# Merge gates as one product of 1024 columns, six pairs of k-tiles by Strassen's seven block products

## The reference, cut to what matters

```
u = rmsnorm(x, norm_w)
proj = u @ w_in                      # 4096 x 24576: a_q a_f a_i a_g c_b c_c c_h c_g (2048 each), g_a g_b (4096 each)
y_a = rmsnorm(hgrn2(a_q, a_f, a_i)) * silu(a_g)
y_b = (c_b * conv3(c_c * c_h)) * silu(c_g)
merged = sigmoid(g_a + bias0) * (y_a @ w_branch_a) + sigmoid(g_b + bias1) * (y_b @ w_branch_b)
out = rmsnorm(x + merged @ w_out, final_norm_w)
```

## Time and profile before

| | us |
|---|---|
| three runs | 2910.37 to 2911.72, median 2911.26 |
| the profiled execution | 2910.26 |
| its span (first to last instruction) | 2908.5 |
| TensorE busy in the span | 2889.1 |
| VectorE busy | 1600.1 |
| ScalarE busy | 1231.9 |
| one merge, period | 131.5 |

### The profile page before, as it was taken

The page is one execution under the profiler, slowest core; times in us unless marked ns, Lnnn a source line. Parts: engine busy times, 40 slices in busy tenths (PEclk is TensorE's granted clock), DMA queues, the critical chain, the costliest instruction groups (busy, mean ns, idle before and its releaser), DMA issues.

```text
span 2908.5 us, 39078 instructions
## 1 busy us (share of the span) xinstructions
PE 2889.1 (99%) x13155; PEld 2399.5 (82%) x13155; DVE 1600.1 (55%) x1794; ACT 1231.9 (42%) x1326; POOL 6.7 (0%) x22
## 2 busy tenths in 40 slices
PE   8999999999999999999999999999999999999998
PEld 7888888888888888888888888888888888888886
DVE  6566666666665554555554454445454454555454
ACT  5443444344434444444444344443444344444443
POOL 0000000000000000000000000000000000000000
PEclk9999999999999999999999999999999999999999
DMA  7555555555556666666566666666666666666665
GB/s 240 181 180 167 174 174 179 166 177 174 176 170 192 192 190 190 192 192 191 189 193 201 195 196 195 197 197 193 196 194 197 194 197 194 197 201 212 219 202 202
DMA packets 426970, 556.63 MB, mean 191 GB/s; under 512 B 25393, under 2 KB 287650, under 8 KB 426914
## 3 DMA queue, kind: packets, MB, share of 16 engines
q1 hardware_dynamic: 426914, 555.90, 61.4%
HBM read 551.61 MB, written 4.19 MB: 191 GB/s over the span
## 4 chain that ended last, share of the span: by engine, by line
PE 99%; DVE 0%; ACT 0%; DMA 0%; ACTq 0%; DVEq 0%; issue 0%; SPq 0%
PE PS L837 32%; PE PS L839 32%; PE PS L838 32%; PE SC L868 1%; PE SC L845 0%; PE SS L868 0%; DMA XS<-in_x 0%; DVE WS L483 0%; PE SS L845 0%; PE OB L878 0%; PE OB L877 0%; PE SC L858 0%; PE OB L876 0%; PE SC L899 0%; PE SC L891 0%; PE SC L907 0%
## 5 line engine op out<-in xcount | busy, mean ns | idle before, releaser
L483 DVE TENSOR_TENSOR WS<-RAW,WS 128x1024 fp32r<-128x1024 f32 x1024 | 1253.7, 1225 | 1247.9 <-ACT WS L314 1226.6
L314 ACT ACTIVATE WS<-RAW 128x1024 fp32r<-128x1024 f32 x1024 | 1084.6, 1060 | 1617.4 <-PE PS L839 1613.6
L837 PE MATMUL PS<-WS,U 128*128 128x512 f32 x3584 | 1408.2, 393 | 2.8 <-DVE WS L483 2.8
L839 PE MATMUL PS<-WS,U 128*128 128x512 f32 x3584 | 1397.3, 390 | 0.0
L838 PE MATMUL PS<-WS,U 128*128 128x512 f32 x3584 | 1396.7, 390 | 0.0
L839 PEld LDWEIGHTS PS<-WS,U 128*128 128x128 f32 x3584 | 673.5, 188 | 140.9
L837 PEld LDWEIGHTS PS<-WS,U 128*128 128x128 f32 x3584 | 673.8, 188 | 140.0 <-issue 3.0
L838 PEld LDWEIGHTS PS<-WS,U 128*128 128x128 f32 x3584 | 674.0, 188 | 135.8
L839 PE MATMUL PS<-WS,Y 128*128 128x512 f32 x512 | 199.4, 389 | 0.0
L837 PE MATMUL PS<-WS,Y 128*128 128x512 f32 x512 | 199.4, 389 | 0.0
L838 PE MATMUL PS<-WS,Y 128*128 128x512 f32 x512 | 199.3, 389 | 0.0
(11 more groups left out here) (158 smaller groups left out, 585.6 us busy)
## 6 DMA issues: line engine op xcount, KB each, us to landing
RAW<-in_w_in SPq DMA_DIRECT2D x1024, 256.0 KB
RAW<-in_w_in SPq DMA_DIRECT2D x256, 512.0 KB
RAW<-in_w_out SPq DMA_DIRECT2D x128, 512.0 KB
RAW<-in_w_branch_a SPq DMA_DIRECT2D x64, 512.0 KB
RAW<-in_w_branch_b SPq DMA_DIRECT2D x64, 512.0 KB
XS<-in_x SPq DMA_DIRECT2D x8, 512.0 KB, 5.5
BIAS<-in_gate_bias SPq DMA_DIRECT2D x16, 256.0 KB, 3.8
XR<-in_x SPq DMA_DIRECT2D x8, 512.0 KB, 4.5
```

The source lines that it names most:

```text
L314: act.activation(WS[s][:, :, 0:OW], RAW[s][:, :, :], ACT.Copy).then_inc(hi_ready, 1)
L483: dve.tensor_tensor(WS[s][:, :, OW:2 * OW], RAW[s][:, :, :], WS[s][:, :, 0:OW], ALU.subtract).then_inc(lo_ready, 1)
L837: pe.matmul(bank, top, w[:, k, 0:OW], start=at_k == 0, stop=False)
L839: op = pe.matmul(bank, low, w[:, k, 0:OW], start=False, stop=at_k == n_tiles - 1)
```

## The change

Gates a and b of a merge become one stream of 16 **units**. A unit is a pair of k-tiles (j, j+16) by 1024 columns (512 of g_a and 512 of g_b): two loads of 512 KB, each one k-tile by 2x512 columns. Ten units are plain (N): four blocks of 128x512 of weights, six matmuls each, 24 in all, summed in the new PSUM tile `QL` (4 banks, in the place of `SC`, `OB`, `SS`). Six units are seven block products (S): the 2x2 blocks (row half by k-tile) times (k-tile by gate) are multiplied in Winograd's form with seven products of three matmuls, 21 in all. The activation sums for them (`SV`, and x21 - x22 in the place of x21's k-tile 0 to 5) are made once, in the last branch; the weight sums on DVE in every S unit. Units come in the order NNSNNSNSNNSNSNSN; the split weights lie in a ring `QS` of 11 blocks, and `block_used` counts the blocks that TensorE has used. Products common to several outputs are collected in `PS[0]` and `PS[1]` and added by `gates_early` and `gates_late`.

Since sums mix the two row halves, the rows must be scaled beforehand: during and after the first branch `U` is rebuilt as (high + low) times 1/rms and split again, in five batches of k-tiles; drains after that are plain copies or products.

`merged` rows go to a DRAM tensor instead of being transposed in the next merge; in the last merge seven of them are loaded back (`MB`), transposed and split. The first merge and the last are written out beside the loop. `x_rms` gets two small multiplications of the identity by 1/rms and TensorE one product with ones, from which a row of 1/rms (`RB`) is made. In the cut below, arguments are shortened where they don't matter; `gates_early` ends with four more additions of 512 columns with a drain after each.

```diff
+UNITS: "NNSNNSNSNNSNSNSN"; N_SEVEN = 6; QRING = 11; AHEAD_UNITS = 2
+NORM_BATCHES = ((0, 8), (8, 16), (16, 24), (24, 28), (28, 32))
# SP
+            def merge(i, first=False, last=False):
+                for u, (_, j) in enumerate(UNITS):
+                    for h in range(2):
+                        load_gates(i, j + KH * h, 2 * u + h, chunk + 2 * u + h)     # waits lo_ready, chunk - 3
+                    if u == 5 and not first:
+                        sp.wait_ge(merged, i)
+                        sp.dma_start(M_DRAM[i - 1], GA).then_inc(spilled, 16)
+                    if u == 9:
...
+                        sp.dma_start(GA[:, 0, :], gate_bias[0, 0, cols].partition_broadcast(P)).then_inc(bias_loaded, 16)
+                        sp.dma_start(GB[:, 0, :], gate_bias[0, 1, cols].partition_broadcast(P)).then_inc(bias_loaded, 16)
                 for n, w in enumerate((w_branch_a, w_branch_b)):
                     for c in range(CB):
                         load_wide(w[0], (i + 1) * OW - OW, c, chunk + 2 * CD + n * CB + c)
+                        at_c = n * CB + c
+                        if last and at_c >= 4 and at_c % 2 == 0:
+                            for m in ((0, 1, 2, 3) if at_c == 4 else (at_c // 2 + 1,) if at_c < 12 else ()):
+                                if m == 0:
+                                    sp.wait_ge(w_used, chunk + 2 * CD)
+                                if m >= 4:
+                                    sp.wait_ge(m_turned, m - 3)
+                                sp.dma_start(MB[m % 4][:, :, :], M_DRAM[m]).then_inc(m_back[m % 4], 16)
# DVE, first branch (ACT: norm_hi copies the high part, 1024 or 2048 columns a batch)
+            def norm_scale(n):
+                dve.wait_ge(w_used, CD + (b + 1) // KC)
+                after()
+                dve.tensor_tensor(t, U[:, a:b, 0:T], U[:, a:b, T:2 * T], ALU.add)
+                after()
+                dve.tensor_tensor(t, t, RB[:, :]..., ALU.mult).then_inc(u_scaled, 1)
+            def norm_lo(n):
+                dve.wait_ge(u_norm_hi, n + 1)
+                dve.tensor_tensor(U[:, a:b, T:2 * T], NT[n % 2]..., U[:, a:b, 0:T], ALU.subtract).then_inc(u_norm, 1)
+                    if first and slot in (10, 12, 14):
+                        norm_scale((slot - 10) // 2)
+                    if first and slot in (11, 13, 15):
+                        norm_lo((slot - 11) // 2)
+                    if last and slot == 10:
+                        seven_sums()          # 8 operations of 768 columns
+                    if last and slot == 12:
+                        seven_lo()
+                if first:                     # after slot 15
+                    norm_scale(3); norm_lo(3); norm_scale(4); norm_lo(4)
# DVE, S unit
+            def seven(i, u, n_th):
+                for t in (s, s + 1):
+                    dve.wait_ge(raw_loaded[t], ...)
+                    dve.wait_ge(block_used, (N_BLOCKS - 1) * i + (n + 6 - QRING + 1))
+                dve.tensor_tensor(two sums, 1024 columns).then_inc(t_sum, 1)
+                after()
+                dve.tensor_tensor(sums[2], sums[0], w22, ALU.add)
+                after()
+                dve.tensor_tensor(sums[3], sums[2], w21, ALU.add).then_inc(t_sum, 1)
+                dve.wait_ge(hi_ready, chunk + 2)
+                dve.tensor_tensor(low parts of 3 blocks).then_inc(lo_ready, 2)
+                for m in range(2):
+                    dve.wait_ge(t_hi, ...)
+                    dve.tensor_tensor(low parts of 2 sums).then_inc(t_ready, 1)
+            def gates_early(i):               # before the lo of the first w_branch_a chunk
+                dve.tensor_tensor(GA[:, 0, :], GA[:, 0, :], GB[:, 0, :], ALU.add)
+                after()
+                dve.wait_ge(block_used, (N_BLOCKS - 1) * i + (FIRST[LAST_S] + 6))
+                dve.tensor_tensor(GB[:, 0, :], a, GB[:, 0, :], ALU.add)
+                dve.tensor_tensor(GA[:, 0, :], e, GA[:, 0, :], ALU.add)
+                after()
...
+            def gates_late(i):                # before the lo of chunk 2
+                dve.wait_ge(w_used, MERGE_CHUNK + MERGE * i + 2 * CD)
+                dve.tensor_tensor(GA[:, :, :], QL[:, 0:2, :], GA[:, :, :], ALU.add)
+                dve.tensor_tensor(GB[:, :, :], QL[:, 2:4, :], GB[:, :, :], ALU.add).then_inc(drained, 1)
+                    lo(chunk + 2 * CD + c, c % RING)
+                    if last and c >= 7 and c % 2 == 1:
+                        turned_lo((c - 7) // 2)     # two operations of 512 columns; ACT: turned_hi after the same hi
+                    if first and 2 <= u < 5:
+                        convolve(NP - 1, u - 2, PS[0][:, 0, :], PS[0][:, 1, :], held=True)   # step 0 increments conv_read
# TensorE
+                        if n_th == 0:         # first S unit
+                            if first:
+                                pe.wait_ge(conv_read, NP)
+                    if last and c % 2 == 0 and c >= 2 * CD + 2:
+                        n = (c - 2 * CD - 2) // 2
+                        if n < NM - 1:
+                            if n > 0: pe.wait_ge(m_ready, n)      # turned_lo(n - 1) is through
+                            pe.wait_ge(m_back[n % 4], n // 4 * 16 + 16)
+                            turn_merged(n, MB[n % 4])
```

More of the change, by code:

```diff
@@ L148, in build @@
         u_ready = sem("u_ready")
+        rms_ready = sem("rms_ready")
+        rms_spread = sem("rms_spread")
+        u_scaled = sem("u_scaled")
+        u_norm_hi = sem("u_norm_hi")
+        u_norm = sem("u_norm")
+        v_sums = sem("v_sums")
+        v_hi = sem("v_hi")
+        v_ready = sem("v_ready")
+        t_sum = sem("t_sum")
+        t_hi = sem("t_hi")
+        t_ready = sem("t_ready")
+        block_used = sem("block_used")
+        conv_read = sem("conv_read")
+        spilled = sem("spilled")
+        m_back = [sem(f"m_back{i}") for i in range(4)]
         fq_turned = sem("fq_turned")
@@ L398, in merge @@
                 group = MERGE_GROUP + 4 * i
[L399 to L420, removed]
+                act.wait_ge(v_ready, 1)
+                n_th = 0
+                for u, (kind, _) in enumerate(UNITS):
+                    if u < AHEAD_UNITS:
+                        continue
+                    if kind == "S":
+                        seven(i, u, n_th)
+                        n_th += 1
+                    else:
+                        for h in range(2):
+                            plain(i, u, h)
@@ new lines, in merge @@
+                for c in range(2 * CB + RING):
+                    if c < RING:
+                        after_gates(i, c)
+                    else:
+                        hi(chunk + 2 * CD + c, c % RING)
+                    if c == RING:
+                        act.wait_ge(drained, group + 2)
+                        act.activation(GA[:, :, :], GA[:, :, :], ACT.Sigmoid).then_inc(merge_gate, 1)
+                        act.activation(GB[:, :, :], GB[:, :, :], ACT.Sigmoid).then_inc(merge_gate, 1)
+                    if last and c >= 7 and c % 2 == 1 and c < 2 * CB + RING + 1:
+                        turned_hi((c - 7) // 2)
@@ L422, in _, with turned_hi @@
+            def turned_hi(n):
+                act.wait_ge(m_turned, n + 1)
+                for j in range(2):
+                    op = act.activation(U[:, 4 * n + 2 * j:4 * n + 2 * j + 2, 0:T], pair(SC[j]), ACT.Copy)
+                op.then_inc(m_hi, 1)
             merge(0, first=True)
@@ L431, in output @@
                         if first and n == 0 and c == MERGED_AT + 2:
[L432 to L435, removed]
+                            turned_hi(NM - 1)
                     if last and n == 1:
@@ L952, in _, with three @@
                 branch(i, CONV_CHUNK, CONV_GROUP, is_conv=True, conv_of=i - 1)
[L954 to L960 removed]
+            def three(bank, top, low, q, start, stop):
+                w = QS[:, q % QRING, :]
+                pe.matmul(bank, top, w[:, 0:OW], start=start, stop=False)
+                pe.matmul(bank, top, w[:, OW:2 * OW], start=False, stop=False)
+                return pe.matmul(bank, low, w[:, 0:OW], start=False, stop=stop)
@@ new lines, in gates @@
+            def gates(i, first):
+                pe.wait_ge(v_ready, 1)
+                pe.wait_ge(y_ready, 2 * NP - 1)
+                pe.wait_ge(drained, MERGE_GROUP + 4 * i - 2)
+                n_th = 0
+                for u, (kind, j) in enumerate(UNITS):
+                    if kind == "S":
+                        if n_th == 0:
+                            pe.wait_ge(drained, MERGE_GROUP + 4 * i)
+                            if first:
+                                pe.wait_ge(conv_read, NP)
+                        seven(i, u, j, n_th)
+                        n_th += 1
+                    else:
+                        plain(i, u, j)
+                    if first and u == 0:
+                        turn_conv(NP - 1, PS[0][:, 0, :], PS[0][:, 1, :])
```

396 lines of the change are left out of this document (293 added, 103 removed).

## The result

The changed kernel takes 2916.64 us (median of 20 runs, 2914.51 to 2921.0) against 2910.78 (20 runs) before: ratio 1.002, 95% interval 1.0014 to 1.0027. That is 5.9 us slower: small, just at the 0.2% that the prediction called distinguishable, but the interval leaves out 1. The prediction's range held the time; its 2913 was 3.6 us short. The profiled execution's span went from 2908.5 to 2915.5 us, by 7.0.

The account below looks back on a forecast made before the run. TensorE bounds the kernel: number of matmuls times 0.2267 us. -32.6 + 14.0 + 0.6 + 0 + 3.0 + 2.0 + 14.9 = +1.9 us, so 2913 us ("the same", chance 0.40); range 2901 to 2929, by its own bounds 2903 to 2923.

Parts of the forecast that it names:

- The gain, 32.6 us: Gates of 8 merges: 21 matmuls for 24 in each S unit, 144 matmuls saved at 0.2267 us, 32.6 us faster.
- block ends cost TensorE: Rival, slower: 656 blocks each change bank and increment a semaphore; 20 ns each is 13 us, 2926; chance 0.10 with other losses.
- S units at no cost: Pairs SN: VectorE works 9.1 of 10.2 us and stays ahead, cover 0.65; loads take 5.2 of 5.7 us; cost 0.
- S units come late: Rival, slower, at the 48 S units: VectorE's slack or load pairs fall short, half a microsecond at tight pairs, 2925; chance 0.26.
- First branch, 14.0: Normalization in the first branch: x_rms 0.5, 11.9 us waited at second branch's chunk 4, slow matmuls behind it 1.6; sum 14.0.
- Last branch 0.6: seven_sums in slot 10 takes VectorE 7.7 us; the `lo` behind it is ready at 11.5, wanted at 10.9: 0.6 us.
- end of the gates 3.0: After each merge's last plain unit, gates_early delays the first w_branch_a chunk's `lo`: 0.4 us each, 8 times, 3.0 (bounds 0 and 8).
- First merge, 2.0: TensorE's first S unit waits for conv_read, as VectorE does its own S unit and two PSUM copies first: 2.0 us.
- Last merge, 14.9: Six turn_merged wait for turned_lo, 1.1 us each; three wait longer for loads, 4.2, 3.7, 3.7: 14.9 (bounds 6.7 and 19).
- a slower clock after these pauses is absorbed: Last merge: slow matmuls behind its pauses add nothing to the 14.9, since the load ends last.
- Eight such at 0.20 more cost 1.6: Behind the first branch's 11.9 us wait, TensorE starts slowly: eight matmuls at 0.20 us more, 1.6 (bounds 0 and 3).
- the row with 0.6 us of idle: Profile row at x_rms where TensorE already waits 0.60 us; after that pause no slow start of matmuls was seen.

Follow-up runs that it names:

- three_of_16: Changed kernel with three units by block products instead of six (375 gate matmuls a merge instead of 366): 2927.9 us, ratio 1.0061 to the kernel before.
- mb_later: Changed kernel with the loads of merged rows 4, 5 and 6 issued two chunks later in the last merge: 2910.89 us, ratio 1.0 to the kernel before.
- last_fix: Changed kernel with merged-row loads two chunks later and each turn_merged one chunk later in the last merge: 2901.02 us, ratio 0.9963 to the kernel before.
- two_sevens: Changed kernel with the same six S units in adjacent pairs SS (NNSSNNSSNNSSNNNN): 2990.41 us (two runs), ratio 1.0274 to the kernel before.

## Why the prediction was right, and by how much it was off

- **The gain, 32.6 us**: right. Nine matmuls a merge measured 2.00 us for 2.04, and the rival "block ends cost TensorE" did not happen.
- **S units at no cost**: right. VectorE's list held to a tenth. The loads were closer than I put them. In the first merge the second load of a pair landed 5.37 us after its own issue and 5.8 after the first one's, with 5.2 assumed and 5.7 allowed, and VectorE began the next S unit 0.15 us behind its period (chain in order of time):

```profile
1579.78 0.39 SPq L300
1580.22 5.37 DMA RP<-in_w_in
1585.67 1.23 DVE QF L926
```

  VectorE waited last for a load before 12 of the 48 S units, but its slack took that up: TensorE's timeline has no such wait before an S block. So the rival "S units come late" stood at the edge and did not happen. The Trainium skill (DMA: Bandwidth & Descriptors, Bandwidth) gives 6.15 us for 1 MB, measured on transfers issued from GpSimd. The pair here, issued from SyncE, took 5.8, a little less than that and more than my 5.2.
- **First branch, 14.0**: measured 16.4. The two pauses are 10.4 and, with the late start behind it, 1.4: 11.8 for 11.9. The slow clock behind them is 2.7 for 1.6. x_rms is 0.9 for 0.5: 0.4 of waiting, and the rest for the new product around 70.5 us, which the prediction didn't count. The slow stretch at the very start, which no term held, is 1.0 longer than in the profile before.
- **Last branch 0.6, end of the gates 3.0**: 0.3 and 3.1 to 3.2.
- **First merge, 2.0**: the pause is 2.0; in this profile 1.6 of slow clock comes on top.
- **Last merge, 14.9**: 15.7. The pauses are 4.85 for 4.2, 1.63 and 3.03 for 3.7 each, and three of 1.1. The loads in them took 6.13, 4.50 and 4.33 us from their issue, where 5.5 was assumed. The second pause is so short because slow matmuls and transposes filled the time that its load took. The stretch of three_of_16, whose clock stayed at 1.00 there, and its second pause show it without them:

```profile
2513.00:2560.00 47.00, 34.66 (x173) 27.63 (x172) 22.34 (x25) 18.31 (x24) 0.00 (x0) 1.00 0.50 169
```
```profile
2526.98 0.65 PE L1172 MATMUL QL<-IDN,MB 128*128 128x128 f32 x4 [3.48 <-DVE U L985]
```

  By differences of starts the second pause is 3.64 us there and 1.63 here. So of the 2.9 us of slow clock some 2.0 came back: "a slower clock after these pauses is absorbed" held for the larger part, and the long first pause makes up the rest of the 15.7. mb_later and last_fix show the two causes of the pauses apart, the loads held behind `turn` and the `turn` that comes before the low parts of the one before.
- **The term that was mis-sized** is the clock. "Eight such at 0.20 more cost 1.6" was taken once, behind the long pause alone. In the profile of the changed kernel it stands at 2.7 + 1.6 + 2.9 = 7.2 us, 5.6 more than was put. The single pauses were together 2.2 us shorter than worked out (26.6 for 28.8), which hid part of it. Before the result, the row with 0.6 us of idle could say nothing of pauses of 2 us, and I set them to zero without a bound.
- **Luck.** That the time was missed by only 3.6 us owes something to this offset, and to the clock itself, which falls behind the same pause in one execution and not in another. The profiled execution of the changed kernel is one with much of it: its first merge and its last merge both have a slow stretch, while three_of_16 has none in either, and its mean granted clock of 0.994 is the lowest among the 20 runs (0.994 to 0.996). How much of it stands in a typical execution isn't settled.

## What to carry to other kernels

Before saving matmuls, list the places where the new work of another engine stands in program order with no chunk ready ahead of TensorE: here 48 S units cost next to nothing and three one-off places cost all that they gave. Spread work that is only needed later, one small batch to each stretch that has idle time. Put a wait in a DMA queue at a point where it is already fulfilled, else every load behind it inherits it. And give the clock behind each pause of TensorE a bound of its own: here a pause of 2 us cost either nothing or 1.6 more, and the pause of 10.4 us cost 2.7 more.

## What the runs showed of the hardware

A pause of 2.0 us was enough to bring TensorE's granted clock to 0.5 (1.2 GHz) for 8 or 9 matmuls of 512 columns, 1.6 us, in 16 of 24 otherwise equal pauses of two_sevens, and in two of eight kernels at the same place in the first merge. After 10.2 us of pause 12 matmuls and the small products behind them were slow. At the cold start the granted clock read 1.00 while matmuls were 0.43 us apart, so there the distance of starts is the better sign.
